# Eight result rows of a group on every sixteenth partition of the inverse's buffer, instead of every fourth of one quarter

## The reference

```python
def hyena_mixer(u, ...):
    z = short_conv(u @ w_in + b_in, conv_w, conv_b)
    x0, x1, v = jnp.split(z, 3, axis=-1)
    s = (v * x1).astype(jnp.float32)
    g = hyena_filter(L, ...)
    n = 2 * L
    y = jnp.fft.irfft(jnp.fft.rfft(s, n=n, axis=1) * jnp.fft.rfft(g, n=n, axis=0)[None],
                      n=n, axis=1)[:, :L]
    y = (y + s * skip.astype(jnp.float32)).astype(u.dtype) * x0
    return y @ w_out + b_out
```

## Time and profile before

| | us |
|---|---|
| median of three runs | 2461.24 (2459.37 to 2461.28) |
| the profiled execution | 2460.01 |
| span of its trace, first to last instruction | 2458.2 |
| PE busy | 2365.6 (96%) |
| DVE busy | 1107.8 (45%) |
| ACT busy | 605.4 (25%) |
| POOL busy | 646.3 (26%) |
| mean granted PE clock | 0.984 |

### The profile page before, as it was taken

How to read it: one execution, slowest core, us unless ns; L and a number is a source line. 1 busy time by engine, 2 the same in 40 slices (tenths; PEclk the granted TensorE clock), 3 DMA queues, 4 the chain that set the end, 5 groups by cost and what they waited for, 6 DMA issues and landing times.

```text
span 2458.2 us, 29269 instructions
## 1 busy us (share of the span) xinstructions
PE 2365.6 (96%) x11692; PEld 1900.3 (77%) x11692; DVE 1107.8 (45%) x1131; ACT 605.4 (25%) x672; POOL 646.3 (26%) x362
## 2 busy tenths in 40 slices
PE   7999998799999999999997999999999999999996
PEld 5766772378888888888886888989897877778885
DVE  6765445352662055413366827363543024500533
ACT  4333313422110010001123626262633011111011
POOL 2221210123333233333342122222222233323321
PEclk9999999899999999999998999999999999999997
DMA  4143239512221223112111202020214221112231
GB/s 155 51 124 127 89 123 342 208 35 84 96 85 43 85 77 102 51 43 69 51 59 36 103 27 77 26 77 26 77 33 172 102 77 56 56 43 67 96 120 68
DMA packets 75331, 211.51 MB, mean 86 GB/s; under 512 B 22006, under 2 KB 25912, under 8 KB 75002
## 3 DMA queue, kind: packets, MB, share of 16 engines
q1 hardware_dynamic: 64794, 172.72, 21.5%
q10 hardware_dynamic: 10464, 37.75, 4.1%
HBM read 165.36 MB, written 40.37 MB: 84 GB/s over the span
## 4 chain that ended last, share of the span: by engine, by line
PE 75%; DVE 3%; ACT 1%; issue 0%; ACTq 0%; DVEq 0%
PE ps L1205 63%; PE ps L538 5%; DVE T L1855 1%; PE ps L1479 1%; PE ps L585 1%; PE ps L604 1%; PE ps L605 1%; PE ps L567 1%; PE ps L606 1%; PE ps L1227 1%; DVE XN L1885 0%; PE ps L1236 0%; PE ps L504 0%; DVE X L2179 0%; DVE H L1878 0%; PE ps L523 0%
## 5 line engine op out<-in xcount | busy, mean ns | idle before, releaser
L1205 PE MATMUL ps<-H,whi 128*128 128x512 f32 x4000 | 1083.9, 393 | 20.6 <-DVE H L1922 10.1
L1205 PEld LDWEIGHTS ps<-H,whi 128*128 128x128 f32 x4000 | 750.9, 189 | 198.1 <-issue 28.9
L1155 POOL CAST whi<-wraw 128x1024 fp32r<-128x1024 f32 x174 | 182.3, 1048 | 1690.4 <-PE ps L1205 842.8
L1205 PE MATMUL ps<-H,wlo 128*128 128x512 f32 x2000 | 618.2, 390 | 0.0
L1157 POOL TENSOR_TENSOR wlo<-wraw,whi 128x1024 fp32r<-128x1024 f32 x178 | 452.2, 2540 | 53.2 <-ACT whi L672 39.3
L1205 PEld LDWEIGHTS ps<-H,wlo 128*128 128x128 f32 x2000 | 376.8, 188 | 79.3
L1205 PE MATMUL ps<-A,whi 128*128 128x512 f32 x1472 | 395.8, 391 | 9.3 <-DVE A L2211 4.9
L1205 PEld LDWEIGHTS ps<-A,whi 128*128 128x128 f32 x1472 | 276.9, 188 | 68.3 <-issue 5.3
L1205 PE MATMUL ps<-A,wlo 128*128 128x512 f32 x736 | 227.4, 390 | 0.0
L1205 PEld LDWEIGHTS ps<-A,wlo 128*128 128x128 f32 x736 | 138.7, 188 | 29.0
L2095 DVE TENSOR_TENSOR T<-ps,T 128x1024 f32<-128x1024 f32 x22 | 26.9, 1224 | 155.8 <-PE ps L1205 155.8
(11 more groups left out here) (336 smaller groups left out, 2307.3 us busy)
## 6 DMA issues: line engine op xcount, KB each, us to landing
wraw<-in_panels SPq DMA_DIRECT2D x181, 512.0 KB, 3.6
mw<-in_modp SPq DMA_DIRECT2D x24, 512.0 KB, 3.6
g<-gsp SPq DMA_DIRECT2D x16, 512.0 KB, 3.7
gr<-g SPq DMA_DIRECT2D x16, 512.0 KB, 12.6
bs<-s SPq DMA_DIRECT2D x16, 512.0 KB, 12.2
YB<-yi ACTq DMA_DIRECT2D x16, 512.0 KB
X<-in_xT SPq DMA_DIRECT2D x4, 1024.0 KB, 7.1
s<-sa SPq DMA_DIRECT2D x8, 512.0 KB, 2.7
```

What stands on the lines that cost most here:

```text
L1155: nc.gpsimd.tensor_copy(whi[:, s, :, :], wraw[:, s, :, :]).then_inc(hi_made, 1)
L1205: last = mm(p[:, c * step:(c + 1) * step], w[:, ws, k, :], operand(act, a, k, c * step, step), start=(q == 0 and w is whi and a == 0), sto ...
```

## The change

`y_rows(g)` named the partitions g%4 + 32(g//4), and from there every fourth up to +28: four groups fill one quarter of 32 partitions. Now it names g, g+16, ..., g+112: every group has one partition in each block of 16. The four DMAs that load the matrix `idft` write its rows in the order that belongs to this: partition 16r + g gets row 8g + r. Each still writes 32 partitions of 64 floats; the source was taken in 8 steps of 4 rows and is now taken in 2 steps of 16.

```diff
         def y_rows(g):
-            return slice(g % 4 + 32 * (g // 4), g % 4 + 32 * (g // 4) + 29, 4)
+            return slice(g, P - GROUPS + 1 + g, GROUPS)
...
-            for a in range(0, P, 32):
-                sp.dma_start(cst[a:a + 32, CST["idft"]:CST["idft"] + HALF],
-                             d["cst"][a:a + 32, CST["idft"]:CST["idft"] + HALF].rearrange("(b r) c -> r b c", r=8)
+            rows = d["cst"][:, CST["idft"]:CST["idft"] + HALF].rearrange("(g r) c -> r g c", r=P // GROUPS)
+            for a in range(0, P // GROUPS, 2):
+                sp.dma_start(cst[a * GROUPS:(a + 2) * GROUPS, CST["idft"]:CST["idft"] + HALF], rows[a:a + 2, :, :]
                              ).then_inc(const_in, 16)
```

## The result

The changed kernel takes 2506.43 us (median of four runs, 2504.7 to 2508.3) against 2460.3 us for the kernel before, measured beside it. The ratio is 1.0188, with a 95% interval of 1.017 to 1.0206. The change makes the kernel 46 us slower.

A forecast was written before the change was run, and what follows sets the result against it. TensorE bounds the kernel overall, DMA the spectral stage from about 400 us. Colliding result writes (+36) and slower loads (+5) give +41 on 2460.0, 2501; the median lies 1.2 us higher: 2502 us, range 2462 to 2535.

The forecast's parts named there:

- the reads in step: Late `YB` transfers: engines reading `yi` 16 partitions apart slow by two or more when they start together.
- pairs: Result writes: engines get in each other's way two by two, a packet takes 0.32 us, a transfer 5.1 us.
- the upper end: Result writes: a packet at the slow stretch's 0.375 us, so 6.0 us for a transfer, +3.45.
- the partly hidden case: Rival, spectral stage: engines alternate load and `YB` packets, only stretches without loads pay; 2466 to 2490 us, chance 0.16.
- stalls: End of the stage: last four old transfers take 3.9 us instead of 2.55; about 5 us already paid.
- the first term of the sum: Result transfers in the spectral stage: the pair price less the 5 us already paid, +36 us.
- The loads: Fuller part of the stage: loads wait for their slowest engine too, some 5 us.
- The waits: Spectral stage: ACT's `yi` copies wait for transfers three groups back, delaying DVE, TensorE and SP's loads; 8.2 us a group.
- The matrix at nothing: Loading the inverse's matrix in new order: below 5 us at worst, cost 0 under some 195 us of cover.
- No effect: Rival: writes are buffered and only reads get in each other's way; 2461 us, chance 0.08.
- faster: Rival: slow stretches come from writes within 32 partitions, and the new spread removes them; 2450 us, chance 0.08.
- 57 GB/s throughout: Rival, much slower: every result transfer at the worst microsecond's rate, 9.2 us each; +101 us, 2563 us, chance 0.06.

The follow-up runs named there:

- the kernels with repeated transfers: Last three transfers made four more times (four rounds) in the kernel before, changed, steps of 8, steps of 1: 2511.52, 2573.79, 2560.97, 2676.31 us.
- steps of 16: The changed kernel's placement, a group's results on partitions 16 apart, against 4 apart in the kernel before: 2506.43 us, ratio 1.0188.
- steps of 8: Against the kernel before, a group's results on every eighth partition of one half of the buffer, matrix order fitted: 2490.59 us, ratio 1.0127.
- steps of 2: Against the kernel before, a group's results on every second partition of a block of 16, matrix order fitted: 2491.57 us, ratio 1.012.
- Steps of 1: Against the kernel before, a group's results on eight neighbouring partitions, matrix in plain order: 2559.14 us, ratio 1.0394.

## Why the prediction was right

The prediction was 2502 us in a range of 2462 to 2535, and 2506.4 was measured. Point by point:

- **The stage is bound by the eight engines that carry the results.** Right in the main: all but 1.6 us was lost between 380 and 515 us, and the share of one half in the stretches with `YB` transfers alone came back in the kernels with repeated transfers. Only its end, where the DMA engines idle from 495 to 504 us, isn't bound by them.
- **Eight engines before and after, the same packets.** Right: from 370 to 512 us q10 has 2153 of its 2176 packets, with the last few behind.
- **Engines 16 partitions apart collide, argued from the reads in step.** The conclusion is right for writes: alone they move 106 GB/s all the time, where the old placement reaches 182. The way to it had some luck. The slow stretches of the kernel before look like the start of a round: 27 packets from 468.1 to 469.6 us are 0.48 us each, too dear for pairs. The start is as slow in every placement, and that reads in step cause it is not shown.
- **The price of a transfer.** I took 5.1 us (a packet of 0.32) and 6.0 us as the upper end. Alone it is 0.31 us for a packet. In the stage the mean is 0.283 us, so 4.5 us for a transfer. Perhaps an engine that is at a load leaves the place to its partner for a while, as in the partly hidden case; no run shows it, and that case's time (2466 to 2490 us) fell.
- **What the old transfers cost.** I set 2.55 us, less 5 us in all for stalls. The mean over the stage was 0.186 us for a packet, 3.0 us for a transfer. So the first term of the sum, +36 us, is nearer to +24 us (16 x (4.5 - 3.0)): it was too large.
- **The loads.** I gave them 5 us. They cost 16 us more of an engine on average: this is the term that was too small. The two errors nearly cancel (36 + 5 against 24 + 16), and that 2502 came so close is luck; the range was the claim.
- **The waits.** I expected ACT to wait for a DMA from the fifth group on, the buffers of `yi` holding up the rest. It did so for two copies only, 9.8 us in all. After that PE waited for `bs`, 26.7 us instead of 5.3, and ACT for PE. The copies came 9.0 us apart instead of 8. So the delay reached PE by the late loads, which I had taken as a side effect.
- **The rest, 6 to 8 us.** The first inverse matmul was expected at 508 us and came at 515.10. From 495 to 504 us the DMA engines idle while PE finishes a group behind the late last `bs`, at first at a clock of 0.71. I had reckoned with engines that are busy to the end.
- **The matrix at nothing, and all that follows moves along.** Right, by the kernel with the matrix alone (0.9995) and by the equal shift of inverse and span, 48.3 us.
- **The rate of the transfers alone.** I expected less than about 105 GB/s and no recovery to 180. It was 105 from 506 to 510 us, and 106 alone.
- **The rivals.** No effect, faster and 57 GB/s throughout: all three fell. The 57 GB/s exist, but with two places and not with four.

**What stays open.** Alone, a transfer with steps of 16 is no dearer than one with steps of 8 (17.5 and 17.0 us for a round). The difference between a round of these and one of before, 5.2 and 4.7 us for three transfers, gives +28 and +25 us for sixteen. For steps of 8 and 2 that is near the loss in the stage (+30 and +31). Steps of 1 fit too: 17.0 us for three transfers, +91 us for sixteen, against +98. Steps of 16 lose 46 us (41 with the destination alone), some 13 to 18 us more than their transfers alone explain.

The traces say where the excess lies. With steps of 8 a packet of results takes 0.264 us in the stage and a megabyte of loads 56.3 us (370 to 497 us), with steps of 16 it is 0.283 and 59.4 us: some 4 us more of each engine for either. The rest goes with the end of the stage, where the DMA engines idle from 495 to 504 us; with steps of 2 they do so for some 4 us (a share of 0.06 from 484 to 488 us), and with steps of 8 their share stays at one half. Why the loads are dearer with steps of 16 is open. The four places of a group lie in both halves there and in one half with steps of 8 and 2, so other loads meet them. That is only an argument: no kernel put four places into both halves in another way, or ran the stage without its loads.

## What to carry to other kernels

Where few partitions of SBUF are the target of a DMA, count the engines that take part and the places that they reach, not how wide the partitions are spread: eight rows 4 apart reached eight places, 16 apart only four, side by side only two. If the stage is bound by its transfers, the price of a packet is the first thing to read, as share x engines x time / packets, in one stretch where a queue is alone and one where it isn't. And a slow stretch elsewhere in the old trace is only a hint at a new pattern's price: here it was also there in every placement. Repeating the transfer by itself in a kernel of its own gave the price directly.

## What the runs showed of the hardware

- Eight DMA engines, each writing 4 KB rows to a partition of its own, moved 182 GB/s at eight places, 105 to 106 at four and 57 at two.
- The first round of transfers began slowly wherever its results went: 0.49 to 0.61 us for a packet in one early microsecond, in all four placements. With eight places the rate was 74 GB/s in the first 1.5 us and reached 182 GB/s later in the same round.
- The loads beside such transfers lost more in latency than in engine time: the median from issue to landing of `bs` went from 12.2 to 20.2 us, and the last one took about 24 us, while a megabyte of loads cost 28% more engine time (46.6 and 59.4 us).
